# Router from the transposed residual in four pieces, routing constants and zero fill made ahead, on one core

## The reference

```python
h = rms_norm(x, g_ffn[l])                       # x * rsqrt(mean(x*x) + eps) * g
logits = ht @ w_router                          # 256 x 8
top_v, top_i = lax.top_k(logits, 2)
top_w = jax.nn.softmax(top_v, axis=-1)
y = (silu(xb @ w_gate[e]) * (xb @ w_up[e])) @ w_down[e]   # xb: the tokens of expert e
x = x + the sum over a token's two experts of top_w * y
out = rms_norm(x, g_final)
```

## Time and profile before

| | |
|---|---|
| median of three runs | 1736.01 us (1734.8 to 1739.36) |
| profiled execution | 1735.96 us, span of its trace 1734.2 us |
| TensorE, VectorE, ScalarE, GpSimd busy | 98%, 78%, 67%, 3% of the span |
| mean granted clock of TensorE | 0.995 |
| DMA | 496.53 MB, mean 286 GB/s |

### The profile page before, as it was taken

How to read it: one execution, slowest core, us unless ns; L and a number is a source line. 1 busy time by engine, 2 the same in 40 slices (tenths; PEclk the granted TensorE clock), 3 DMA queues, 4 the chain that set the end, 5 groups by cost and what they waited for, 6 DMA issues and landing times.

```text
span 1734.2 us, 28399 instructions
## 1 busy us (share of the span) xinstructions
PE 1703.9 (98%) x9640; PEld 1482.0 (85%) x9640; DVE 1351.3 (78%) x1451; ACT 1166.9 (67%) x1361; POOL 52.4 (3%) x75
## 2 busy tenths in 40 slices
PE   8999999999999999989999999999999999999998
PEld 7988999999988888968888888888888888888886
DVE  6775575455457754769899998999999999999998
ACT  5565645444444665458787878787887878787876
POOL 2000000000000000010000000000000000000100
PEclk9999999999999999999999999999999999999999
DMA  9543376666656433799999999999999999999993
GB/s 338 176 114 112 130 244 185 183 191 185 189 160 203 122 110 110 239 362 398 375 372 387 376 382 377 368 396 377 365 394 373 374 385 376 382 375 374 369 383 143
DMA packets 169469, 496.53 MB, mean 286 GB/s; under 512 B 15168, under 2 KB 17232, under 8 KB 168896
## 3 DMA queue, kind: packets, MB, share of 16 engines
q1 hardware_dynamic: 165168, 480.57, 76.9%
q0 software_dynamic: 4240, 15.14, 2.7%
HBM read 482.54 MB, written 13.11 MB: 286 GB/s over the span
## 4 chain that ended last, share of the span: by engine, by line
PE 92%; ACT 3%; DVE 2%; DMA 2%; issue 1%; POOL 0%; SPq 0%; DVEq 0%; ACTq 0%
PE ps L1831 85%; PE ps L2259 1%; ACT probs L1099 1%; PE ps L2069 1%; PE ps L2052 1%; DMA expert_rows<-held 1%; PE ps L2039 1%; DMA raw<-in_w_mem_kv 0%; PE ps L2041 0%; DVE wlo L1297 0%; ACT probs L1091 0%; ACT whi L966 0%; PE ps L2266 0%; DMA normed_rows<-gates 0%; PE ps L1883 0%
## 5 line engine op out<-in xcount | busy, mean ns | idle before, releaser
L1297 DVE TENSOR_TENSOR wlo<-raw,whi 128x1024 fp32r<-128x1024 f32 (+1 forms) x768 | 913.0, 1219 | 277.5 <-ACT whi L966 253.2
L966 ACT ACTIVATE whi<-raw 128x1024 fp32r<-128x1024 f32 (+1 forms) x768 | 800.0, 1057 | 315.4 <-PE ps L1831 300.1
L1831 PE MATMUL ps<-whi,xg_hi 128*128 128x512 f32 x896 | 352.6, 394 | 3.2 <-DVE xg_lo L1711 2.0
L1831 PE MATMUL ps<-wlo,xg_hi 128*128 128x512 f32 x896 | 349.8, 390 | 0.0
L1831 PE MATMUL ps<-whi,xg_lo 128*128 128x512 f32 x896 | 349.2, 390 | 0.0
L1831 PE MATMUL ps<-hT_hi,whi 128*128 128x256 f32 x896 | 258.9, 289 | 3.0 <-ACT gates L976 3.0
L1831 PE MATMUL ps<-hT_lo,whi 128*128 128x256 f32 x896 | 253.5, 283 | 0.0
L1831 PE MATMUL ps<-hT_hi,wlo 128*128 128x256 f32 x896 | 253.3, 283 | 0.0
L1831 PEld LDWEIGHTS ps<-whi,xg_hi 128*128 128x128 f32 x896 | 168.7, 188 | 37.7 <-DVE wlo L1297 3.8
L1831 PEld LDWEIGHTS ps<-wlo,xg_hi 128*128 128x128 f32 x896 | 168.4, 188 | 35.6
L1831 PEld LDWEIGHTS ps<-whi,xg_lo 128*128 128x128 f32 x896 | 168.8, 188 | 34.2
(11 more groups left out here) (335 smaller groups left out, 2039.1 us busy)
## 6 DMA issues: line engine op xcount, KB each, us to landing
raw<-in_w_down_exp SPq DMA_DIRECT2D x216, 512.0 KB, 5.8
raw<-in_w_gate_exp SPq DMA_DIRECT2D x210, 512.0 KB, 5.5
raw<-in_w_up_exp SPq DMA_DIRECT2D x120, 512.0 KB, 5.4
raw<-in_w_in SPq DMA_DIRECT2D x72, 512.0 KB, 3.6
vM<-in_w_up_exp SPq DMA_DIRECT2D x56, 512.0 KB, 5.6
kM<-in_w_up_exp SPq DMA_DIRECT2D x48, 512.0 KB, 6.5
raw<-in_w_gate_dense SPq DMA_DIRECT2D x28, 512.0 KB, 4.0
raw<-in_w_up_dense SPq DMA_DIRECT2D x28, 512.0 KB, 3.9
```

The lines of the kernel that those rows point to most:

```text
L966: s.activation(whi[n % SPLIT][:, 0:w], raw[tile(key)][:, 0:w], ACT.Copy).then_inc(chunk_hi, 1)
L1297: v.tensor_tensor(wlo[n % SPLIT][:, 0:w], raw[tile(key)][:, 0:w], whi[n % SPLIT][:, 0:w].bitcast(F32), ALU.subtract).then_inc(chunk_split, 1)
L1831: ins = mm(o, lhsT, rhs, start=start and i == 0, stop=stop and i == 2, skip_group_check=True)
```

## The change

The router's weights are multiplied by the norm's gain `g_ffn[1]` in layer 0 (eight small DMAs, one product on GpSimd), and are split to `wr_hi` and `wr_lo` before layer 0's attention instead of in its projections. The router product then takes the transposed residual: the order of the logits of a token doesn't depend on its norm factor, and the difference of the two largest is multiplied by `rstd` before the exponential. The residual's first half is transposed within the output product, the second behind it, and the product runs in four pieces between transposes and identity products. `norm_apply` of tile 1 moves behind the lower parts on VectorE. Upper and lower parts of expert chunk 0, and the upper part of chunk 1, move into the mixer's end. The zero fill has a source of its own, `zero_rows`, and is issued in layer 0 ahead of the dense loop; ScalarE and VectorE wait for it at the head of layer 1. The routing constants are made during layer 1's branch products. Counts get a full event of their own in `ps[2]`; the one-hot, the counts and the route table are in a new order on VectorE, with fewer instructions; the fill of `back` is dropped. The core of the diff, indentation cut:

```diff
+if l == 0:
+    for k in range(KD):
+        pool.dma_start(wr_gain[:, k:k + 1], A["g_ffn"][1, P * k:P * (k + 1)].unsqueeze(1)).then_inc(router_loaded, 16)
+    pool.wait_ge(router_loaded, 16 * (KD + 1))
+    nc.gpsimd.tensor_tensor(wr[:, :, :], wr[:, :, :], wr_gain.unsqueeze(2).to_broadcast([P, KD, EXPERTS]),
+                            ALU.mult).then_inc(wr_scaled, 1)
...
-    rstd_of(2 * l + 2)
-    load_gain(2 * l + 3, A["g_mix"][1] if l == 0 else A["g_final"])
-    if l == 0:
...
+    if l:
+        wait_full(pool, ("oT", l, len(units) - 1))
         nc.gpsimd.memset(ones[:, :], 1.0).then_inc(routing_constants, 1)
...
+        nc.gpsimd.iota(route[:, :, 3:3 + 2 * NT:2], pattern=[[0, 2 * EXPERTS + 1], [P, NT]], base=0,
+                       channel_multiplier=1, allow_small_or_imprecise_dtypes=True).then_inc(routing_constants, 1)
...
-        nc.gpsimd.iota(iotaS[:, :], pattern=[[1, SLOTS]], base=0, channel_multiplier=0,
+        nc.gpsimd.iota(iotaS[:, :], pattern=[[1, SLOTS]], base=1, channel_multiplier=0,
...
+    rstd_of(2 * l + 2)
+    load_gain(2 * l + 3, A["g_mix"][1] if l == 0 else A["g_final"])
+    if l == 0:
...
+        nc.gpsimd.memset(zero_rows[:, :], 0.0).then_inc(y_cleared, 1)
+        pool.wait_ge(y_cleared, 1)
+        pool.dma_start(expert_rows[SLOTS * EXPERTS:, :].rearrange("(b p) d -> p b d", p=SLOTS),
+                       zero_rows[:, :].unsqueeze(1).to_broadcast([SLOTS, EXPERTS + 1, D])).then_inc(y_zeroed, 16)
+        pool.wait_ge(y_zeroed, 16)
 pool.wait_ge(norm_done, NT * 5)
 pool.dma_start(normed_rows.rearrange("(t p) d -> p t d", p=P), normed).then_inc(rows_stored, 16)
 pool.wait_ge(rows_stored, 16)
-pool.wait_ge(normed_split, 1)
-pool.wait_ge(hT_split, tl.after("hT_split", ("hT", 3, 3)))
-nc.gpsimd.memset(y_rows, 0.0).then_inc(y_cleared, 1)
-pool.wait_ge(y_cleared, 1)
-pool.dma_start(expert_rows[SLOTS * EXPERTS:, :].rearrange("(b p) d -> p b d", p=SLOTS),
-               y_rows.unsqueeze(1).to_broadcast([SLOTS, EXPERTS + 1, D])).then_inc(y_zeroed, 16)
...
+if l:
+    for key in moe_loop[0:AHEAD]:
+        hi_of(key, 0)
 for half in range(2):
     for t in range(NT):
         eng.wait_ge(x_added, tl.after("x_added", ("out", l, half, t)))
         square(x, half, t)
+    if l:
+        transposed_part(("hT", 2 * l + 1), half)
...
-transposed(("hT", 2 * l + 1))
+    transposed(("hT", 2 * l + 1))
...
-s.activation(normed_hi[:, :, :], normed, ACT.Copy).then_inc(normed_hi_ready, 1)
 copy_out(("router",), logitsT[:, :], ps[2][0:EXPERTS, 0:TOK])
+eng.wait_ge(norm_done, NT * 5)
+for half in range(2):
+    cols = slice(512 * half, 512 * (half + 1))
+    s.activation(normed_hi[:, :, cols], normed[:, :, cols], ACT.Copy).then_inc(normed_hi_ready, 1)
...
+eng.wait_ge(turns_ready, 1)
+turns = s.value_load(turns_i[0:1, 0:1], min_val=EXPERTS, max_val=2 * EXPERTS)
 with s.Fori(0, turns) as e:
...
-eng.wait_ge(y_zeroed, 16)
+eng.wait_ge(rows_stored, 16)
 s.activation(y_rows, ps[2][:, :], ACT.Copy, scale=slot_w[:, 0:1]).then_inc(y_copied, 1)
...
+    if n and l:
+        lo_of(moe_loop[0], 0)
...
         if n and t == 0:
+            if l:
+                for i in range(2):
+                    transposed_piece(("hT", 2 * l + 1), i)
             norm_mean(2 * l + 2, 0)
-norm_apply(2 * l + 2, 0, x, normed)
-norm_mean(2 * l + 2, 1)
 if l == 0:
...
+    transposed(("hT", 1))
+else:
+    norm_apply(4, 0, x, normed)
+    for i in range(2, 4):
+        transposed_piece(("hT", 3), i)
+    norm_mean(4, 1)
+    norm_apply(4, 1, x, normed)
...
 step(v.tensor_copy(top_f[:, :, :], top_i[:, :, :]))
-v.tensor_tensor(pair_d[:, :], top8[:, :, 1], top8[:, :, 0], ALU.subtract).then_inc(diff_ready, 1)
-for r in range(2):
-    for t in range(NT):
-        ins = v.tensor_scalar(hot[:, r, t, :], iota8[:, :], top_f[:, t, r:r + 1], None, ALU.is_equal)
+for rank in range(2):
+    ins = v.tensor_tensor(hot[:, rank, :, :], iota8[:, :].unsqueeze(1).to_broadcast([P, NT, EXPERTS]),
+                          top_f[:, :, rank:rank + 1].to_broadcast([P, NT, EXPERTS]), ALU.is_equal)
 step(ins)
 v.tensor_tensor(routed[:, :, :], hot[:, 0, :, :], hot[:, 1, :, :], ALU.add).then_inc(masks_ready, 1)
+step(v.tensor_tensor(pair_d[:, :], top8[:, :, 1], top8[:, :, 0], ALU.subtract))
+v.tensor_tensor(pair_d[:, :], pair_d[:, :], rstd[:, :], ALU.mult).then_inc(diff_ready, 1)
+def normed_rest(half):
+    eng.wait_ge(normed_hi_ready, half + 1)
+    cols = slice(512 * half, 512 * (half + 1))
+    v.tensor_tensor(normed_lo[:, :, cols], normed[:, :, cols], normed_hi[:, :, cols].bitcast(F32),
+                    ALU.subtract).then_inc(normed_split, 1)
+normed_rest(0)
+wait_full(eng, ("rank",))
+eng.wait_ge(masks_ready, 1)
+both = logits[:, :, :].rearrange("p t e -> p (t e)")
+step(v.scalar_tensor_tensor(both, ps[3][:, 0:NT * EXPERTS], 1.0, routed[:, :, :].rearrange("p t e -> p (t e)"),
+                            ALU.add, ALU.mult))
+for t in range(NT):
+    ins = v.tensor_scalar(onehot_next[:, t, :], iotaS[:, :], logits[:, t, 0:1], None, ALU.is_equal)
+ins.then_inc(routed_sem, 1)
+normed_rest(1)
+eng.wait_ge(psum_full[2], tl.after("psum_full2", "counts"))
+step(v.tensor_reduce(most[:, :], ps[2][:, NT * EXPERTS:(NT + 1) * EXPERTS], AX.X, ALU.max))
+step(v.tensor_scalar(turns_f[:, :], most[:, :], SLOTS + 0.5, float(EXPERTS), ALU.is_gt, ALU.mult))
+step(v.tensor_scalar(turns_f[:, :], turns_f[:, :], float(EXPERTS), None, ALU.add))
+v.tensor_copy(turns_i[:, :], turns_f[:, :]).then_inc(turns_ready, 1)
+by_turn = logits[:, :, :].rearrange("p t e -> p e t")
+for turn in range(2):
+    v.tensor_scalar(route[:, EXPERTS * turn:EXPERTS * (turn + 1), 0:NT], by_turn, float(SLOTS * turn),
...
 eng.wait_ge(ratio_ready, 1)
 step(v.tensor_scalar(pair_d[:, :], pair_e[:, :], 1.0, None, ALU.add))
...
-wait_full(eng, ("rank",))
-both = logits[:, :, :].rearrange("p t e -> p (t e)")
-step(v.tensor_scalar(both, ps[3][:, 0:NT * EXPERTS], 1.0, None, ALU.add))
-step(v.tensor_tensor(both, both, routed[:, :, :].rearrange("p t e -> p (t e)"), ALU.mult))
+for rank in range(2):
+    ins = v.tensor_tensor(route_w[:, rank, :, :], hot[:, rank, :, :],
+                          pair_w[:, rank, :].unsqueeze(2).to_broadcast([P, NT, EXPERTS]), ALU.mult)
+step(ins)
...
-step(v.tensor_reduce(most[:, :], ps[3][:, NT * EXPERTS:(NT + 1) * EXPERTS], AX.X, ALU.max))
-step(v.tensor_copy(cur_next[:, :], route[:, 0, :]))
...
-for t in range(NT):
-    v.tensor_copy(back[:, P * t:P * (t + 1)], ones[:, :])
+    ins = v.tensor_tensor(route[:, EXPERTS * turn:EXPERTS * (turn + 1), 2:2 + 2 * NT:2],
+                          route_w[:, 0, :, :].rearrange("p t e -> p e t"),
+                          route_w[:, 1, :, :].rearrange("p t e -> p e t"), ALU.add)
+step(ins)
+v.tensor_copy(cur_next[:, :], route[:, 0, :]).then_inc(routed_sem, 1)
...
-turn_starts(0)
+lo_of(moe_loop[1], 0)
...
+def keep_busy(n, spare=None):
...
+def turned_rows(a, t):
+    if t == 0:
+        wait_free(pe, ("hT", 3, a, "area"))
+    pe.wait_ge(x_added, tl.after("x_added", ("out", 1, a, t)))
+    for k in range(4):
+        c = TOK * k + P * t
+        ins = nc.tensor.transpose(ps[a][:, c:c + P], x[:, t, P * (4 * a + k):P * (4 * a + k + 1)], ident[:, :])
+    if t == NT - 1:
+        ins.then_inc(psum_full[a], 1)
+def router(i):
+    if i == 0:
+        pe.wait_ge(wr_split, 1)
+        wait_free(pe, ("router",))
+    wait_piece(("hT", 3), i)
+    for k in range(2 * i, 2 * (i + 1)):
+        ins = three(ps[2][0:EXPERTS, 0:TOK], wr_hi[:, k, :], wr_lo[:, k, :], hT_hi[:, k, :], hT_lo[:, k, :],
+                    k == 0, k == KD - 1, True)
+    if i == 3:
+        ins.then_inc(psum_full[2], 1)
...
+    if l and t == 0 and c == 2:
+        for tt in range(NT):
+            turned_rows(0, tt)
 if t == 0:
...
-transposes(("hT", 2 * l + 1), 2 * l + 2)
+turned_rows(1, 0)
+router(0)
+turned_rows(1, 1)
+router(1)
+keep_busy(3, ps[3][:, 0:P])
+router(2)
+router(3)
...
+keep_busy(3)
 wait_free(pe, ("router_T",))
...
 ins.then_inc(psum_full[2], 1)
-keep_busy(12)
+keep_busy(6)
 pe.wait_ge(masks_ready, 1)
 wait_free(pe, ("rank",))
...
-mm(ps[3][:, 16:24], ones[:, :], routed[:, 1, :], start=False, stop=True).then_inc(psum_full[3], 1)
+mm(ps[3][:, 8:16], earlier[:, :], routed[:, 1, :], start=False, stop=True).then_inc(psum_full[3], 1)
+wait_read(pe, ("router_T",))
+mm(ps[2][:, 16:24], ones[:, :], routed[:, 0, :], start=True, stop=False)
+mm(ps[2][:, 16:24], ones[:, :], routed[:, 1, :], start=False, stop=True).then_inc(psum_full[2], 1)
...
+if k % (KD // 2) == 0:
+    pe.wait_ge(normed_split, k // (KD // 2) + 1)
...
-keep_busy(8)
-pe.wait_ge(normed_split, 1)
+keep_busy(4)
 pe.wait_ge(routed_sem, 1)
...
+pe.wait_ge(routed_sem, 2)
 slots_back(ps[1])
-keep_busy(4)
+keep_busy(3)
 pe.wait_ge(turns_ready, 1)
```

More of the change, by code:

```diff
@@ L263, in build_tally @@
             psum(("rank",), 3, free=("turns_ready", "turns"))
+            tl.add("psum_full2", "counts")
             tl.add("routed", "first")
+            tl.add("routed", "first_slots")
             for half in range(2):
```

(48 more changed lines are left out.)

74 lines of the change are left out of this document (33 added, 41 removed).

## The result

The changed kernel takes 1724.97 us (median of four runs, 1724.94 to 1725.28); the kernel before took 1735.4 us on the same chip (1734.71 to 1739.36). The ratio is 0.993, 95% interval 0.9908 to 0.9951: faster, by 0.5 to 0.9%. The profiled executions (spans 1734.2 and 1723.2 us) are 11.0 us apart, where 9.0 was forecast, and the medians 10.4. The forecast time was 1727.0, in a range from 1724.3: the measured 1724.97 lies in it, but the ratio applied to 1736.01 gives 1723.9, just under its low end.

A forecast was written before the change was run, and what follows sets the result against it. The serial chain from the mixer to expert chunk 4, where TensorE's waits end, was taken to set the time. Chunk 4 10.0 us earlier, less 1.0 for the clock, gives 9.0: 1735.96 to 1727.0, range 1724.3 to 1731.

The forecast's parts named there:

- first expert matmul: TensorE's start on the experts, forecast at 760.2 against 767.80 before: 7.6 us gained.
- chunk 4: Fourth-numbered expert weight chunk: TensorE starts it at 766.4 against 776.37, or 767.4 with the clock fall.
- row store lands: Store of the normed rows, issued at about 750.5 with 6.33 us to land: 757, before ScalarE's copy at 761.3.
- The sum: Total gain up to chunk 4: 10.0 us less 1.0 for the clock, 9.0; bounds 7.0 and 11.4.
- eight transposes: First half of the residual turned inside the mixer's last output product: 0.98 us, paid in full.
- Register read: Reading the turn number into a register behind the gather, ahead of the experts: costs 1.43 us, until 758.2.
- The clock: Idle 1.7 us ahead of the experts brings half clock for 3.5 us: 1.0 us lost.
- Rival (2): New gaps before router, masks or gather bring half clock; each stretch costs up to 1.8 us, total 1730; chance 0.12.
- Rival (3): Row store lands behind the router-released loads, at 765; chunk 4 at 768.5, time 1728.1; chance 0.06.
- The fill in the dense stage: Zero fill moved beside layer 0's dense loads: costs zero, upper bound 5.4 us.
- The router's gain: Eight 0.5 KB DMAs and one GpSimd product beside the opening loads: zero, at most 3.7 us.
- The constants: They leave GpSimd's path between last norm and row store (1.1 us), which nothing on the path waits for.

The follow-up runs named there:

- second repeat: The changed kernel run again unchanged, the second time, for comparison on the same chip as other runs: 1725.35 us.
- the router back: Changed kernel with transposes and router product on the normed rows behind both norms again, without the gain in the weights: 1727.96 us.
- the fill alone: Kernel before, with only the zero fill moved to layer 0 with its own source, and ScalarE's copy waiting for the row store: 1731.78 us.
- the constants back: Changed kernel with the eight routing constants made on GpSimd between the last norm's gain load and the row store, as before: 1731.9 us.
- the fill back: Changed kernel with the zero fill from `y_rows` back behind the row store and ScalarE's copy waiting on it: 1745.27 us.
- the longer idle stretch: Changed kernel without the three identity products behind the slots' way back, ahead of the first expert matmul: 1726.04 us.

## Why the prediction was near, and where it was off

The direction and the mechanism were right, and so were most sizes. Forecast and measured, step by step, in us on the time line:

| step | forecast | measured |
|---|---|---|
| last add of the mixer | 743.80 | 743.17 |
| the router's last matmul, end | 748.4 | 747.68 |
| VectorE's copy of the logits | 749.65 | 748.79 |
| gather | 753.45 | 752.44 |
| TensorE idle ahead of the experts | 1.7 | 0.98 |
| first expert matmul | 760.2 | 758.53 |
| chunk 4, clock kept | 766.4 | 765.35 |
| chunk 4, clock fallen | 767.4 | did not fall |
| row store lands | 757 | 761.89 |

*The sum.* Chunk 4 started 2.05 us ahead of the forecast. Of this 1.0 is the fall of the clock that was put in and did not come. The rest is 1.05: the first expert matmul came 1.67 early, and 0.62 of that was given back in the wait for chunk 4 behind the row store, which the sum had at nothing. So the nearness of the sum owes something to errors that cancel.

*The starting point.* The mixer's last product reached its first add 0.55 us earlier than before (736.83 for 737.38), where the change does nothing; the opening differs by such amounts from one execution to the next (the last add of the changed kernel: 743.17, and 743.94 in its second repeat). So 0.55 of the 1.67 is no work of the change. The eight transposes took 0.87 in the chain of waits, for 0.98.

*Register read.* It was taken at 1.43; the issue time ahead of VectorE's next long instruction behind it is 0.99 here and 0.77 to 1.39 in the other traces of the new order. That is 0.44 of the 1.67; the remaining 0.6 is spread over small steps.

*The clock: the step that failed.* "I take the fall" (1.0 lost) rested on an idle stretch of 1.7 us ahead of the first expert matmul. It came out at 0.98: TensorE was done 1.0 us before the forecast, but VectorE 1.7, the shorter register read among them. The price was near: with the stretch made 1.79 the clock fell, and 1.2 us was lost behind it in that trace. What the prediction could not say is when a fall comes. A gap of 2.07 was followed by one before, and gaps of 2.07 with the router back or with the fill alone moved were not. The clock also bears on the low end of the range, which was set against one execution: of 43 runs of the kernel before in these sessions 25 took under 1738 us (median 1735.2) and 18 took 1738.3 to 1744.6 (median 1741.6), 16 of the latter at a mean granted clock of 0.990 to 0.994, but 6 of the former too. That long falls of the clock make these runs is argued from the clock and from the run with the constants back, not seen in a trace of one. The changed kernel has no such second group: its twelve runs, repeats included, lie between 1724.8 and 1726.8. That this is because its gaps are gone is not shown: with the fill alone moved and a gap of 2.07 left, none of ten runs is above 1735.8 either. So by the medians the gain is 10.4 us in the first session and 11.4 and 13.6 in the two with a repeat, and the sum was made against the profiled execution.

*Rival (2), half clock in the router or the gather,* did not come, but was priced too low for the gather: up to 1.8 us for a stretch, where the run with the constants back shows 5.

*Rival (3), the row store,* was half true. The prediction's row took 6.33 us, from a trace in which the store went out ahead of the router's loads; put behind them it landed at 761.9, 12.12 us after its issue, past the 761 that the prediction named as a sign against itself, and ScalarE's copy waited 2.52. Its price at chunk 4 was 0.62 us in this execution and 0.2 in each repeat, for 1.1 forecast, since VectorE was nearly as late. With the fill still behind it TensorE waited 17.8 us.

*The fill in the dense stage: nothing,* as forecast, though it landed in 23.5 us at a DMA share of 0.99. The prediction has the fill's 16.42 us in a stretch where the loads took all of the bandwidth. By the trace of before 382 GB/s were moved in it, 6.3 MB, and 4.7 MB of these, three quarters, were the fill's own. The dense loads between 255 and 300 took 7.3 us to land in the median and 12.5 at most, for 4.3 and 7.3 before; the tiles' lead covers both. The rule of the Trainium skill ("DMA: Bandwidth & Descriptors", "Queues, rings and completion order") that the engines alternate between queues agrees in kind: the loads went on landing beside the fill.

*The router's gain: nothing that can be told.* Its product was done at 38.5 and waited for by nothing; an idle stretch of 1.30 us at 44.86 in one trace is absent in both repeats and back at 0.71 and 0.48 in two others. The eight loads took 4.2 us to issue and 4.6 more until the product, for 4 KB, all hidden. The rule of the Trainium skill ("DMA: Bandwidth & Descriptors", "Rules for kernel authors") of one descriptor per element can be neither confirmed nor refuted here: between 28 and 40 us GpSimd's queue has 400 packets for 144 before, 32 more for each load of 128 elements, and no row tells how many descriptors a packet holds.

*The constants: wrong.* They were costed at nothing, as a piece of GpSimd's way to the row store. That VectorE waits for all eight ahead of the logits was left out. Before, they were ready at 748.9 for a copy at 754.22; with that copy at 748.8 and the constants where they were, VectorE stood idle for 2.42 us.

## What to carry to other kernels

The gains of edits to one chain of transfers don't add up: here, by the spans, one edit alone gave 5.0 us (differences from run to run and of the clock are part of it), the other alone cost 9.5, and both gave 11.0. A landing time read from one trace holds for what else was in flight there. Before an edit is costed at nothing, look at what its work would be late for once the other edits have moved their consumers earlier. Cheap matmuls in a stretch in which TensorE waits can keep the clock through a serial part: the 19 identity products were worth 2.7 us here by the medians.

## What the runs showed of the hardware

- The fall of the granted clock does not follow from the length of a single gap. It stayed at 1.00 behind 2.07 us in two kernels (the fill alone, the router back), fell behind 2.07 in the kernel before and behind 1.79 in another, and for one and the same kernel (the constants back) the mean clock was 0.996 in two runs and 0.992 in five, 5 us apart.
- What a fall costs depends on the work behind it: 1.2 us in front of the expert products, some 5 us in front of the gather, on which two other engines wait.
- The same store of 1 MB landed in 5.4 to 7.0 us where the loads released by the router were issued behind it (before, the fill alone, the router back), and in 10.3 to 13.3 us where they were issued ahead of it (the changed kernel, its repeats, the fill back, the longer idle stretch, the constants back). In two halves issued 1.7 us apart, the halves took 5.1 and 10.4 us.
